# A two-layer hybrid model on one core: the pair loop of the experts written out, and four pieces of work put in another place

## What is computed

```python
def moe_swiglu(x, router_w, w1, w3, w2):
    logits = (x @ router_w).astype(F32)
    top_val, top_idx = lax.top_k(logits, TOP_K)          # 2 of 8
    top_w = jax.nn.softmax(top_val, axis=-1)
    gates = jnp.sum(jax.nn.one_hot(top_idx, N_EXPERTS, dtype=F32) * top_w[..., None], axis=-2)
    y = jnp.zeros(x.shape, F32)
    for e in range(N_EXPERTS):                           # 1024 -> 3584 -> 1024 each
        y = y + gates[..., e:e + 1] * swiglu(x, w1[e], w3[e], w2[e]).astype(F32)
    return y.astype(x.dtype)

h = h + moe_swiglu(rms_norm(h, ffn_norm_w[1]), ...)
gate = jax.nn.sigmoid(rms_norm(h, ple_norm_w[1]) @ ple_gate[1])
h = h + (p[1] @ ple_proj[1]) * gate
return rms_norm(h, final_norm_w)
```

## Time and profile before

| | us |
|---|---|
| median of three runs (lowest, highest) | 1507.92 (1506.56, 1508.27) |
| the profiled execution | 1504.48 |
| its span in the profile | 1502.7 |
| TensorE busy in the span | 1447.2 (96%) |
| VectorE busy | 1261.4 (84%) |
| ScalarE busy | 1065.5 (71%) |
| DMA, bytes moved and mean rate | 467.60 MB, 311 GB/s |
| mean granted TensorE clock | 0.988 of full speed |

### The profile page before, as it was taken

One profiled execution on the slowest core, in us unless ns is written; L12 is line 12 of the kernel. 1 busy time (PEld: TensorE's weight loads), 2 busy tenths in 40 slices (PEclk: granted clock), 3 DMA queues, 4 the chain that ended last, 5 costly groups with the idle time before them and its releaser, 6 DMA issues.

```text
span 1502.7 us, 22251 instructions
## 1 busy us (share of the span) xinstructions
PE 1447.2 (96%) x8114; PEld 1227.8 (82%) x8114; DVE 1261.4 (84%) x1238; ACT 1065.5 (71%) x1073; POOL 186.7 (12%) x200
## 2 busy tenths in 40 slices
PE   9999999999999997999999999999999998999997
PEld 8999899998999976777887777888776776877885
DVE  5977765656697768999888999979999999999994
ACT  6566433435766656888778888778898888888774
POOL 2662100000156200000001000100001001002100
PEclk9999999999999998999999999999999999999999
DMA  8561574555546137999999999999999999999990
GB/s 351 186 206 60 206 278 168 183 210 214 180 165 196 73 141 268 420 423 422 393 367 354 421 423 422 387 366 383 412 423 422 412 424 422 420 422 421 420 353 29
DMA packets 84899, 467.60 MB, mean 311 GB/s; under 512 B 16704, under 2 KB 26304, under 8 KB 30784
## 3 DMA queue, kind: packets, MB, share of 16 engines
q1 hardware_dynamic: 80816, 451.03, 76.2%
q0 software_dynamic: 3984, 15.22, 2.7%
HBM read 452.71 MB, written 13.52 MB: 310 GB/s over the span
## 4 chain that ended last, share of the span: by engine, by line
PE 66%; DVE 11%; DMA 11%; issue 6%; ACT 5%; SPq 0%; POOL 0%; DVEq 0%; ACTq 0%
PE ps L2469 8%; PE ps L2470 8%; PE ps L2473 8%; PE ps L2462 7%; DMA raw<-in_experts 7%; PE ps L2464 7%; PE ps L2463 7%; DVE wlo L880 6%; PE ps L2954 4%; PE ps L2958 4%; ACT whi L876 3%; PE ps L2968 3%; DMA work<-in_experts 2%; PE ps L2982 1%; DMA raw<-in_stream 1%
## 5 line engine op out<-in xcount | busy, mean ns | idle before, releaser
L880 DVE TENSOR_TENSOR wlo<-raw,whi 128x2048 fp32r<-128x2048 f32 x373 | 848.6, 2302 | 68.2 <-ACT whi L876 67.0
L876 ACT CAST whi<-raw 128x2048 fp32r<-128x2048 f32 x373 | 708.1, 1915 | 74.9 <-DMA raw<-in_experts 68.6
L2469 PE MATMUL ps<-whi,xh 128*128 128x512 f32 (+3 forms) x588 | 227.4, 388 | 3.3 <-DVE xl L1672 1.7
L2470 PE MATMUL ps<-whi,xl 128*128 128x512 f32 (+3 forms) x588 | 224.4, 383 | 0.0
L2462 PE MATMUL ps<-xh,whi 128*128 128x256 f32 x656 | 186.7, 285 | 0.0
L2464 PE MATMUL ps<-xh,wlo 128*128 128x256 f32 x656 | 183.8, 280 | 0.0
L2463 PE MATMUL ps<-xl,whi 128*128 128x256 f32 x656 | 183.7, 280 | 0.0
L2473 PE MATMUL ps<-wlo,xh 128*128 128x512 f32 (+3 forms) x588 | 154.4, 384 | 0.6 <-DVE wlo L880 0.6
L2958 PE MATMUL ps<-wlo,xh 128*128 128x512 f32 x464 | 131.9, 406 | 6.2 <-DVE wlo L880 5.8
L2954 PE MATMUL ps<-whi,xh 128*128 128x512 f32 x464 | 134.9, 413 | 2.8 <-DVE xh L2082 2.8
L2469 PEld LDWEIGHTS ps<-whi,xh 128*128 128x128 f32 x588 | 110.4, 188 | 29.0 <-ACT whi L876 4.5
(11 more groups left out here) (418 smaller groups left out, 2047.4 us busy)
## 6 DMA issues: line engine op xcount, KB each, us to landing
raw<-in_experts SPq DMA_DIRECT2D x288, 1024.0 KB, 9.7
raw<-in_stream SPq DMA_DIRECT2D x85, 1024.0 KB, 5.5
work<-in_experts SPq DMA_DIRECT2D x48, 1024.0 KB, 9.7
y_rows<-work POOLq DMA_DIRECT2D x1, 4096.0 KB, 18.6
m_rows<-work SPq DMA_DIRECT2D x2, 768.0 KB, 4.6
work<-x_inv_rows SPq DMA_DIRECT2D x2, 768.0 KB, 5.4
work<-xt_rows SPq DMA_DIRECT2D x2, 768.0 KB, 7.0
y_rows<-work POOLq DMA_DIRECT2D x1, 1280.0 KB, 22.0
```

The lines of the kernel that those rows point to most:

```text
L876: nc.scalar.copy(upper_slot(n), landed_slot(n)).then_inc(s_hi, 1)
L880: nc.vector.tensor_tensor(lower_slot(n), landed_slot(n), upper_slot(n).bitcast(F32), ALU.subtract).then_inc(s_lo, 1)
L2469: pe.matmul(out, xu, wu, start=start, stop=False)
L2470: return pe.matmul(out, xd, wu, start=False, stop=False)
```

## The change

1. The loop over two pairs is written out on TensorE, ScalarE and VectorE (`for i in range(PAIRED)`), so that waits compare with constants there. SyncE and GpSimd keep theirs.
2. In layer 1's mixer ScalarE and VectorE do one more split: ScalarE between the second squares and the LATE columns, VectorE behind the LATE columns, so ahead of the router. VectorE has one split less behind the table.
3. VectorE copies the slot list behind one split, and does the others after it.
4. In block 2 of a small item ScalarE copies B ahead of `pair_upper` of block 1.
5. In the tail VectorE lowers the LATE columns ahead of the last split.

```diff
--- before.py
+++ after.py
@@ -1406,6 +1406,8 @@
                 if L:
                     split.ahead(1)
                 squares_of(3 * L + 1, 1)
+                if L:
+                    split.ahead(1)
                 turned_residual(3 * L + 1, LATE)
                 if L == 0:
                     split.behind(("WO", L, 1, 1))
@@ -1519,13 +1521,16 @@
                         split.behind(("B", ph, j - 1), now)
                     else:
                         split.ahead(1, now)
+                    if j == 2:
+                        kept(mg[j % 2], ("B", ph, j), now)
                     pair_upper(ph, j - 1, now)
                     if j == 1:
                         split.ahead(ITEM_LEAD - OVER - 1, now)
                     if j != 2:
                         kept(ms[j % 2], ("A", ph, j), now)
                     split.behind(("A", ph, j), now)
-                    kept(mg[j % 2], ("B", ph, j), now)
+                    if j != 2:
+                        kept(mg[j % 2], ("B", ph, j), now)
                     if j < NJ - 1:
                         split.behind(("B", ph, j), now, most=3)
                 split.behind(("B", ph, NJ - 1), now, most=1)
@@ -1588,8 +1593,8 @@
             split.behind(("LG",))
             split.behind(("A", "first", 0))
             split.behind(("B", "first", 0))
-            split.begin("to_whole", through_pair)
-            with act.Fori(0, PAIRED) as i:
+            for i in range(PAIRED):
+                split.begin("to_whole", through_pair)
                 rest_of_small("to_whole", Now(PAIRS, i))
                 rest_of_item("to_small", Now(PAIRS, i))
             split.begin("small", through_run)
@@ -2012,6 +2017,8 @@
                     turned_residual(3 * L + 1, (EARLY, LATE)[m])
                 if L == 0:
                     split.behind(("WO", L, 1, 1))
+                else:
+                    split.ahead(1)
 
             def ple(L, items=None):
                 turned_residual(3 * L + 2, EARLY, items)
@@ -2254,7 +2261,6 @@
                 nc.vector.tensor_reduce(of_rank[:, a], chosen[:, a], AX_X, ALU.add).then_inc(st.sem, st.up())
             step()
             nc.vector.tensor_copy(table[0:1, 0:NI + 1], tabf[0:1, 0:NI + 1]).then_inc(s_tab, 1)
-            split.ahead(1)
             item, place_in, g = (of_rank[:, a].rearrange("p k b -> p (k b)") for a in range(3))
             for k in range(TOPK):
                 for b in range(NB):
@@ -2263,10 +2269,11 @@
                     ins = nc.vector.tensor_scalar(item_token[:, n, :], cc("item"), item[:, n:n + 1], cc("token", b, 1),
                                                   ALU.is_equal, ALU.mult)
             ins.then_inc(s_places, 1)
+            split.behind(("LG",), most=1)
+            filled(dve, ("SL",))
+            nc.vector.tensor_copy(slot_token[:, :], bank(("SL",), 0, NI)).then_inc(s_free["v"], 1)
             split.behind(("LG",))
             split.behind(("A", "first", 0))
-            filled(dve, ("SL",))
-            nc.vector.tensor_copy(slot_token[:, :], bank(("SL",), 0, NI)).then_inc(s_free["v"], 1)
 
             def result_rows():
 
@@ -2361,12 +2368,12 @@
                     turned_residual(5, EARLY, it)
                     for b in range(NB):
                         add_to_residual(("SC", b, 1), b, 1, it)
+                    turned_residual(5, LATE, it)
                     split.behind(("YY", ph, 1), it)
-                    turned_residual(5, LATE, it)
 
             split.behind(("B", "first", 0))
-            split.begin("to_whole", through_pair)
-            with dve.Fori(0, PAIRED) as i:
+            for i in range(PAIRED):
+                split.begin("to_whole", through_pair)
                 rest_of_small("to_whole", Now(PAIRS, i))
                 rest_of_item("to_small", Now(PAIRS, i))
             split.begin("small", through_run)
@@ -3155,7 +3162,7 @@
             slot_tokens()
             pe.wait_ge(s_free["v"], tiles.start[PAIRS]["v"])
             pe.wait_ge(s_free["a"], tiles.start[PAIRS]["a"])
-            with pe.Fori(0, PAIRED) as i:
+            for i in range(PAIRED):
                 rest_of_small("to_whole", Now(PAIRS, i))
                 rest_of_item("to_small", Now(PAIRS, i))
             pe.wait_ge(s_free["v"], tiles.start[RUN]["v"])
```

## The result

| | us |
|---|---|
| kernel before, median of 5 runs (lowest, highest) | 1508.27 (1506.56, 1513.43) |
| changed kernel, median of 5 runs | 1496.73 (1495.97, 1497.28) |
| ratio, 95% interval | 0.9914 [0.9898, 0.9929] |
| its profiled execution, and its span | 1496.99, 1495.3 |
| mean granted TensorE clock (before 0.988) | 0.997 |

A forecast was written before the change was run, and what follows sets the result against it. The expert part was taken as a chain of stages short of bytes or TensorE, winnable only where both stood still. 5.7 + 2.5 + 0.5 + 0.5 = 9.2 us less, 1507.92 to 1498.7, range 1491.5 to 1504.5.

The forecast's parts named there:

- no rival: Three were named: head start given back (8%, 1502.4 us), bytes decide all (6%, 1506.5), small loop stops fitting (6%, 1512).
- Term 1: Way into the pair loop: earlier slot copy and split start merge and VectorE's products sooner; 5.7 us, between 4.6 and 7.2.
- The chain of the prediction: Way into the pair loop: first merge and VectorE's first product 4.6 us earlier, then its 1.36 us idle time gone: 5.9.
- from there VectorE is busy nearly without a break, so it carries the gain on: First pair round, behind VectorE's first product and the split after it: the 5.9 us won there would last.
- the first rival: Head start given back in the first round by VectorE's backlog or falling clock: gain 5.5 us, 1502.4; chance 8%.
- Term 2: End of the pair loop's first pass: written out, TensorE's jump back and its pause go; 2.5 us, between 0 and 4.3.
- the comparison of two rounds: Two small rounds, whole round's end to last block's merge, 87.37 us with the jump and 84.84 without, priced it at 2.5.
- the sign "84 to 85 in the second": Second pair round: 84 to 85 us between first and last merge would show the prediction right.
- Term 3: Block 2 of small rounds: copying B2 earlier removes TensorE's 2 us pause before third merges; 0.5 us, between 0 and 3.
- the cover for term 1: Block 2 in the pair rounds: the edit protects VectorE's head start there, where the merge had no such pause; not priced.
- Term 4: Tail: LATE columns ahead of the last split end TensorE's 0.52 us wait; 0.5 us, between 0 and 0.6.

The follow-up runs named there:

- e9: The change with the early split ahead of the router undone, VectorE's split again ahead of the list's places, early slot copy kept; 1500.89 us, ratio 0.9942 to the kernel before.
- e5: The changed kernel again, unchanged, in another set of runs beside the kernel before; 1497.04 us, ratio 0.9928.
- e10: The change with the tail's old order: VectorE splits the last gate half ahead of the LATE columns; 1500.03 us, ratio 0.9934 to the kernel before.
- e1: The change with the pair loop put back on TensorE, ScalarE and VectorE; 1503.28 us, ratio 0.9948 to the kernel before.
- e6: The kernel before with TensorE's pair loop alone written out, ScalarE and VectorE keeping their jumps; 1505.53 us, ratio 0.9987.
- e3: The change with block 2's old order, ScalarE's copy of B behind the upper cast again; 1498.84 us, ratio 0.9926 to the kernel before.
- e11: The kernel before with one edit alone, the slot copy behind one split instead of three; 1505.38 us, ratio 0.9977.
- e4: The kernel before again, unchanged, for a second profile and more runs; 1509.31 us, ratio 0.9999.
- e8: The kernel before with products left out, TensorE's loop body 1815 instructions; only its jump back is read: 6255 ns.
- e12: The kernel before with more products left out, TensorE's loop body 1293 instructions; only its jump back is read: 238 ns.

## Why the prediction was right

The direction, the median (1496.73 for 1498.7) and the range were right, and no rival came in full. By its own steps, all counted from the addition at 548.31 and 549.16:

**Term 1, 5.7 us.** (The chain of the prediction ends at 5.9 us; why 5.7 was taken it does not say.) The added split costs 0.5 us at the first up-product (23.6 us, in e9 without it 23.1), as worked out. The merge comes at 33.8 instead of 38.75 us: 5.0 us for the 4.6 forecast. It ran at full clock, in 1.97 us for 1.89. VectorE's first product is at 37.95 instead of 42.9, 4.9 for 4.6, and the split behind it 6.4 us earlier for 5.9. The chain was right, link by link. But in this execution the lead does not stay: at the round's last merge it is 122.28 - 117.66 = 4.6 us, and the distance from first to last merge was 83.87 us where I forecast 82.5. What gave way is the step "from there VectorE is busy nearly without a break, so it carries the gain on": from 598 us ScalarE waits for loads (1.65 and 1.41 us), VectorE for ScalarE, and the round runs at 412 GB/s where the first one before ran at 383, a mild form of the first rival.

How far that step holds differs between executions of the same code. ScalarE's waits for loads in that round add up to 3.1 us in the change, 2.8 in e5, 1.7 in e10 and 1.2 in e1, which have the same code so far, and there are none of 0.8 us or more in e9, which lacks the early split; the distance from first to last merge is 83.9, 83.8, 83.1, 82.6 and 82.3 us, and the lead over the kernel before at the last merge 4.6, 4.4, 6.7, 6.9 and 5.9. The forecast's 82.5 and 5.7 lie among these. Of the four with the same code, e10 and e1 are those whose first products ran at 2.4 GHz. So what TensorE's clock does ahead of the first merge goes with how much of term 1 arrives. The prediction had no term for it, and that its 5.7 lies in the middle is in that respect luck.

At the start of the second round (805.88 against 810.48, the end of TensorE's whole item before) the lead of the change's profile is 5.45 us.

**Term 2, 2.5 us.** From there to the last merge of the second round the lead grows to 349.54 - 342.56 = 7.0 us, so by 1.5 us, the difference of 87.37 and 85.84. Undoing it cost 1.9 to 3.6 us, doing it alone gave 2.0 in the median and 0.7 to 1.0 in the profile. So the size, 2.5, is not refuted, and 1.5 is what this pair of profiles shows. The step that was wrong is the comparison of two rounds, 87.37 with the jump and 84.84 without: freed of its jump the pair round takes 85.84, in e5, e6 and e10 86.0 to 86.4, so at least 1 us of its length was never the jump's, and the sign "84 to 85 in the second" was missed by that. That TensorE held 2048 instructions, as the page "Runtime: NRT & Kernel Launch" of the Trainium skill (section "Instruction fetch mechanics") says, was never needed for the sum, and the trace now disagrees with it: 1815 stalled. Its remark on two pages of 256 instructions is contradicted too, by 1293 and 1027 without a stall.

**Term 3, 0.5 us.** From 7.0 us at the end of the second round the lead goes to 573.93 - 566.24 = 7.7 at the last merge of the first small one, and stands at 7.4 at the last transposes: 0.4 us beside my 0.5. As the cover for term 1, which the prediction said it would be and did not price, it does more: without it pauses of 1.86 us stand in both pair rounds (e3; in e11 2.02 and 1.03 us), and the undoing cost 1.0 to 1.4 us in these profiles, a size that their spread leaves open.

**Term 4, 0.5 us.** 0.8 us, by the last column of the table; besides the gap of 0.52 us, the products behind it start sooner.

Together 5.45 + 1.5 + 0.4 + 0.8 = 8.2 us for 9.2 in the change's first profile, and 7.8 to 9.9 over the three. By the profiles the edits are worth more together than apart: the slot copy alone 1.6 to 1.9 us and TensorE's loop alone 0.7 to 1.0, while undoing them in the change costs 3.7 to 5.4 and 1.9 to 3.6. The medians, with intervals this wide, neither confirm nor refute it. e11 and e6 show a way for it to happen: behind the edit that was made alone, a pause that another edit removes grows (from 0.19 to 2.02 us at e11's third merge, from 0.26 to 1.86 at e6's).

**What stays open.** The medians moved by 11.5 and 10.8 us, 1 to 4 us more than the profiles show. The sum was made against an execution 3.4 us under the median, and I took that distance to stay; in the changed kernel it did not. Over all runs the lowest of the kernel before (86 executions, e4's among them) is 1502.81, that of the change (11) 1495.27: 7.5 us, near the profiles' value, though with so many fewer executions the change's lowest may not have been seen (e10, the change but for 0.8 us in the tail, has 1494.83). Some of that is the early stretch at a lower clock, which both have: e8 and e12, with the old way into the pair loop, had their addition at 554.1 and 555.6. The profiles of before, e4, e6 and e11 had it at 548.3 to 548.5 and so show nothing of it. The mean granted clock, which is on record for every execution, goes with the time inside one kernel: e10's two fastest executions (1494.8 and 1494.9 us) had 0.998 and 0.999, its two slowest (1503.9 and 1506.9) 0.992 and 0.993. But the profiled execution of the kernel before was usual in this, 0.988 where the others had 0.982 to 0.992. Whether the rest comes from the pauses of the kernel before, each followed by slow products of a length that varies, was not shown: e11 took the longest away, and its runs still spread over 10.6 us.

## What to carry to other kernels

When an engine's queue holds work for later ahead of a tiny result that another engine stands waiting for, put the tiny result first; here it was worth the wait, the clock that fell behind it, and the loads that the stopped engine did not release, but only up to where the loads themselves bound. Judge such a set of edits together, since a pause that is left can swallow the lead that another edit made. Count from a shared operation behind the last unchanged stage, not from totals, when single executions differ by more than the term in question, and look for a second execution of the same code before you read a term of 1 us: a stretch at the lower clock behind the shared operation moved this one by 1.3 us.

## What the hardware showed that was not expected

TensorE's jump back cost 238 to 249 ns for bodies of 1293 and 1027 instructions, and 5.8 to 6.6 us for 1815 and 2139, so the limit lies between 1293 and 1815, below what I had assumed. The first 550 us of the same code took up to 10 us more in one execution than in another, in e5 with a granted clock of 0.63 in a stretch where another had 1.00. And the length of a pause alone does not tell whether the clock falls: the first up-product of the change stands behind 2.82 us of idle time and its first four products take 2.08 us, part of them at 1.2 GHz; in e10 the same products behind the same pause take 1.20, at 2.4 GHz. In e3 the third merges of the two pair rounds stand behind the same 1.86 us and take 2.00 and 3.67 us. Once the slot copy no longer holds TensorE up, such a stretch ahead of it lands on the path, with 1.3 us at the first merge. e10's row:

```profile
575.61 1.20 PE L2961 MATMUL ps<-whi,xh 128*128 128x512 f32 x4 [2.81 <-DVE xh L2089]
```
